# One block instead of two at the head of a two-layer hybrid kernel: vectors, turned inputs and the first modulated input

## The reference, cut to what matters

```python
def adaln(cv, w, b):
    return jax.nn.silu(cv) @ w + b

def modulate(x, shift, scale):
    return x * (1.0 + scale) + shift

def hgrn_lower_bounds(logits):
    p = jax.nn.softmax(logits.astype(jnp.float32), axis=0)
    return jnp.clip(jnp.cumsum(p, axis=0) - p[0], 0.0, 1.0)
...
    p_lat = jnp.split((h_lat @ w_in).astype(jnp.float32), split_at, axis=-1)
    p_ctx = jnp.split((h_ctx @ w_in).astype(jnp.float32), split_at, axis=-1)
```

## Time and profile before

| what | value |
|---|---|
| median of 3 runs | 4275.97 us (4269.83 to 4277.84) |
| profiled execution, its own time | 4269.11 us |
| its span, first to last instruction | 4267.2 us |
| mean granted TensorE clock over the span | 0.929 of full speed |
| PE busy | 3724.2 us, 87% |
| PEld (weight loads) busy | 3004.4 us, 70% |
| DVE busy | 1755.2 us, 41% |
| ACT busy | 1060.2 us, 25% |
| POOL busy | 231.3 us, 5% |

### The profile page before, as it was taken

The page is one execution under the profiler, slowest core; times in us unless marked ns, Lnnn a source line. Parts: engine busy times, 40 slices in busy tenths (PEclk is TensorE's granted clock), DMA queues, the critical chain, the costliest instruction groups (busy, mean ns, idle before and its releaser), DMA issues. The chain is left out here.

```text
span 4267.2 us, 52183 instructions
## 1 busy us (share of the span) xinstructions
PE 3724.2 (87%) x22306; PEld 3004.4 (70%) x22306; DVE 1755.2 (41%) x1933; ACT 1060.2 (25%) x1465; POOL 231.3 (5%) x126
## 2 busy tenths in 40 slices
PE   3999567979796999999998699568979869999997
PEld 2888445548785888888886588445458758888886
DVE  3111657655424323323334321667556243333334
ACT  1000232446405111111112300232456141111113
POOL 2000003002000000000000000003012000000000
PEclk6999778989898999999999899779989989999998
DMA  5532523022312111111112522422031311211111
GB/s 190 120 88 74 212 92 109 7 82 66 136 52 74 45 45 29 29 44 44 29 32 92 144 84 90 167 98 61 6 110 51 119 40 45 59 44 44 51 38 43
DMA packets 300024, 318.71 MB, mean 75 GB/s; under 512 B 42479, under 2 KB 266331, under 8 KB 299611
## 3 DMA queue, kind: packets, MB, share of 16 engines
q1 hardware_dynamic: 274234, 267.43, 21.1%
q0 software_dynamic: 6912, 30.15, 2.3%
q10 hardware_dynamic: 18720, 18.88, 1.3%
HBM read 247.78 MB, written 71.59 MB: 75 GB/s over the span
## 5 line engine op out<-in xcount | busy, mean ns | idle before, releaser
L491 PE MATMUL psum<-h_hi,f_whi 128*128 128x512 f32 (+1 forms) x1760 | 482.0, 371 | 43.2 <-DVE f_wlo L1114 43.2
L491 PE MATMUL psum<-h_lo,f_whi 128*128 128x512 f32 (+1 forms) x1760 | 481.3, 371 | 0.0
L491 PE MATMUL psum<-h_hi,f_wlo 128*128 128x512 f32 (+1 forms) x1760 | 481.3, 371 | 0.0
L491 PE MATMUL psum<-h_hi,w_hi 128*128 128x512 f32 (+1 forms) x1392 | 369.1, 368 | 99.0 <-DVE w_lo L636 67.8
L491 PEld LDWEIGHTS psum<-h_hi,f_whi 128*128 128x128 f32 x1760 | 308.7, 188 | 102.5 <-DVE f_wlo L1114 43.6
L491 PE MATMUL psum<-h_lo,w_hi 128*128 128x512 f32 (+1 forms) x1392 | 367.2, 367 | 0.0
L1120 DVE SCALAR_TENSOR_TENSOR y<-psum,mods,y 128x1024 f32<-128x1024 f32 (+1 forms) x264 | 260.4, 1015 | 258.4 <-PE psum L491 257.5
L491 PE MATMUL psum<-h_hi,w_lo 128*128 128x512 f32 (+1 forms) x1392 | 366.0, 366 | 0.0
L491 PEld LDWEIGHTS psum<-h_lo,f_whi 128*128 128x128 f32 x1760 | 308.5, 188 | 59.0
L491 PEld LDWEIGHTS psum<-h_hi,f_wlo 128*128 128x128 f32 x1760 | 308.4, 188 | 59.0
L491 PEld LDWEIGHTS psum<-h_hi,w_hi 128*128 128x128 f32 x1392 | 239.4, 190 | 146.0 <-issue 42.1
(11 more groups left out here) (267 smaller groups left out, 5295.6 us busy)
## 6 DMA issues: line engine op xcount, KB each, us to landing
f_raw<-in_w_ffn_in SPq DMA_DIRECT2D x88, 512.0 KB, 6.1
ada_w<-in_w_ada SPq DMA_DIRECT2D x30, 1024.0 KB, 10.9
w_raw<-in_w_in SPq DMA_DIRECT2D x48, 512.0 KB, 5.3
proj_cm<-lin_stage POOLq DMA_DIRECT2D x38, 640.0 KB, 4.2
f_raw<-in_w_ffn_out SPq DMA_DIRECT2D x44, 512.0 KB, 3.8
ada_w<-in_w_ada ACTq DMA_DIRECT2D x18, 1024.0 KB, 5.6
na_qk<-proj_cm SPq DMA_DIRECT2D x48, 320.0 KB, 8.0
hg_pj<-proj_cm SPq DMA_DIRECT2D x20, 640.0 KB, 8.8
```

The source lines that it names most:

```text
L491: ins = nc.tensor.matmul(out[:, t0:t0 + tn], w, h[:, t0:t0 + tn], start=start and n == 0, stop=stop and n == 2)
```

## The change

`setup` and `turn_in` become one function, `front`, with one block.

- SP issues the 16 small loads first (the identity third), then all ten tile loads (those from the fifth on wait for the transposes of the tile four before), then the stores, two tiles in each: five stores of 1024 KB.
- ACT issues the first four `w_ada` pieces at the start, ahead of its Exp and its Silu.
- PE makes the transposes of the vectors and `head_wide`, then waits for `s_done`, which DVE gives with `c_wide`; from there its list is the old one.
- DVE has the same small steps in another order: `head_mean` early, so that `head_wide`'s products run beside the other steps, and `head_wide` and `c_wide` last.
- The modulated input has three buffers, which lie in the memory of `x_rows`. DVE makes the even blocks (`tensor_scalar`), ACT the odd ones (`Identity` with scale and bias); ACT makes all `h_hi`, DVE all `h_lo`. POOL has nothing in the block.
- All semaphores of the block but those of `ModulationTiled` come from the pool.

The diff (the bodies of `setup` and `turn_in`, taken out, are printed above and are cut here, as are the counts at the end):

```diff
@@ -145,90 +145,6 @@
 V_ROWS = 94
-def setup(k):
...
 class Modulation:
@@ -394,45 +310,81 @@
...
-def turn_in(k, h_hi, h_lo, mod_ranges):
...
+def front(k, h_hi, h_lo, mod_ranges):
+    nc, a = k.nc, k.a
     ROWS_IN = 4
     with ExitStack() as st:
...
+        sem = k.stage_sems(st)
+        vec_rows = k.sb(st, "vec_rows", [V_ROWS, P])
+        ada = k.sb(st, "ada_rows", [DEPTH * MB, P])
+        tmp = k.sb(st, "lb_tmp", [P, 8, 4])
+        rows = k.sb(st, "x_rows", [P, ROWS_IN * D])
         xc = k.sb(st, "x_cm", [P, KB, NT])
-        hm = k.sb(st, "h_mod", [P, 2, NT])
         mod = ModulationTiled(k, st, 4, 5, mod_ranges)
         n_m = len(mod.pieces)
...
+        HM = 3
+        s_in = [sem(f"x_loaded{s}") for s in range(ROWS_IN)]
+        (s_con, s_vt, s_v, s_e, s_hm, s_hw, s_done, s_out, s_t, s_x, s_md, s_ma, s_hi, s_lo) = (sem(x) for x in (
+            "rows_loaded", "rows_turned", "vec_step", "lb_exp", "head_mean", "head_wide", "vectors_done", "x_stored", "x_turned", "x_copied",
+            "modulated_dve", "modulated_act", "h_hi", "h_lo"))
+        def row_tile(t):
+            return rows[:, t % ROWS_IN * D:(t % ROWS_IN + 1) * D]
+        def hm(j):
+            return rows[:, j % HM * NT:(j % HM + 1) * NT]
...
+        n = [0]
         with nc.Block() as block:
             @block.sync
             def _(sp):
                 def load(t):
                     if t >= ROWS_IN:
                         sp.wait_ge(s_t.h, s_t.at(t - ROWS_IN + 1))
...
+                    src = a["x"][0, t * P:(t + 1) * P] if t < SEQ // P else a["ctx"][0, t * P - SEQ:(t + 1) * P - SEQ]
+                    sp.dma_start(row_tile(t), src).then_inc(s_in[t % ROWS_IN].h, 16)
+                for dst, src in (
+                    (vec_rows[V_C:V_C + 8], a["c"].rearrange("a (j p) -> (a j) p", p=P)),
+                    (vec_rows[V_C + 8:V_C + 16], a["c_ctx"].rearrange("(j p) -> j p", p=P)),
+                    (k.ident[:], a["c_ident"]),
+                    (vec_rows[V_LNG:V_LNG + 32], a["ln_g"].rearrange("l w (j p) -> (l w j) p", p=P)),
+                    (vec_rows[V_LNB:V_LNB + 32], a["ln_b"].rearrange("l w (j p) -> (l w j) p", p=P)),
+                    (vec_rows[V_LBL:V_LBL + 8], a["hgrn_lb_logits"].rearrange("l d (j p) -> (l d j) p", p=P)),
+                    (ada[:], a["b_ada"].rearrange("l (j p) -> (l j) p", p=P)),
+                    (k.mean_d[:], a["c_mean_d"]), (k.mean_h[:], a["c_mean_h"]), (k.rot[:], a["c_rot"]),
+                ):
+                    sp.dma_start(dst, src).then_inc(s_con.h, 16)
+                for row, name in ((V_QN, "gqa_q_norm"), (V_KN, "gqa_k_norm"), (V_HN, "hgrn_norm")):
+                    for half in range(2):
+                        sp.dma_start(vec_rows[row:row + DEPTH, half * HD:(half + 1) * HD], a[name]).then_inc(s_con.h, 16)
+                for t in range(TT):
                     load(t)
...
-                    sp.wait_ge(s_x.h, s_x.at(t + 1))
-                    sp.dma_start(k.x_dram[:, :, t * P:(t + 1) * P], xc[:, :, t * P:(t + 1) * P]).then_inc(s_out.h, 16)
-                    if t + ROWS_IN < TT:
-                        load(t + ROWS_IN)
...
+                for t in range(0, TT, 2):
+                    sp.wait_ge(s_x.h, s_x.at(t + 2))
+                    sp.dma_start(k.x_dram[:, :, t * P:(t + 2) * P], xc[:, :, t * P:(t + 2) * P]).then_inc(s_out.h, 16)
+                sp.wait_ge(s_out.h, s_out.at(16 * TT // 2))
             @block.tensor
             def _(pe):
+                pe.wait_ge(s_con.h, s_con.at(16 * 16))
+                nc.tensor.transpose(k.psum[:, 0, 0:V_ROWS], vec_rows[:], k.ident[0:V_ROWS, 0:V_ROWS])
+                nc.tensor.transpose(k.psum[:, 1, 0:DEPTH * MB], ada[:], k.ident[0:DEPTH * MB, 0:DEPTH * MB]).then_inc(s_vt.h, 1)
+                pe.wait_ge(s_hm.h, s_hm.at(1))
+                for c in range(3):
+                    for i in range(4):
+                        ins = nc.tensor.matmul(k.psum[32 * c:32 * c + 32, 2, i * P:(i + 1) * P], k.head_mean[:, i], k.ident[:], start=True, stop=True)
+                ins.then_inc(s_hw.h, 1)
+                pe.wait_ge(s_done.h, s_done.at(1))
                 for t in range(TT):
...
+                    pe.wait_ge(s_in[t % ROWS_IN].h, s_in[t % ROWS_IN].at(row_copied(t)))
                     if t >= 2:
                         pe.wait_ge(s_x.h, s_x.at(t - 1))
                     for j in range(KB):
                         ins = nc.tensor.transpose(k.psum[:, 2 * (t % 2) + j // 4, (j % 4) * P:(j % 4 + 1) * P],
...
+                                                  row_tile(t)[:, j * P:(j + 1) * P], k.ident[:])
                     ins.then_inc(s_t.h, 1)
                     for u in range(n_m * t // TT, n_m * (t + 1) // TT):
                         mod.product(pe, u)
@@ -442,6 +394,39 @@
             @block.vector
             def _(dve):
+                def step(ins):
+                    ins.then_inc(s_v.h, 1)
+                    n[0] += 1
+                    dve.wait_ge(s_v.h, s_v.at(n[0]))
+                dve.wait_ge(s_vt.h, s_vt.at(1))
+                step(nc.vector.tensor_copy(k.vecs[:, 0:V_ROWS], k.psum[:, 0, 0:V_ROWS]))
+                lg = k.vecs[:, V_LBL:V_LBL + 8].rearrange("p (l q) -> p l q", l=DEPTH)
+                step(nc.vector.tensor_tensor(tmp[:, 4], lg[:, 0], lg[:, 1], ALU.max))
+                step(nc.vector.tensor_tensor(tmp[:, 0:2], lg, tmp[:, 4:5].to_broadcast([P, 2, 4]), ALU.subtract))
+                step(nc.vector.tensor_copy(k.b_ada[:], k.psum[:, 1, 0:DEPTH * MB]))
+                step(nc.vector.memset(k.head_mean[:], 0.0))
+                for i in range(4):
+                    ins = nc.vector.tensor_copy(k.head_mean[:, i, 2 * i:2 * i + 2], k.mean_h[:, 0:P:HD])
+                ins.then_inc(s_hm.h, 1)
+                step(nc.vector.memset(k.eps[:], EPS))
+                step(nc.vector.memset(k.eps_dn[:], EPS / ALPHA ** 2))
+                step(nc.vector.memset(k.c_wide[:], 0.0))
+                step(nc.vector.tensor_tensor(k.c_pick[:], k.ident[:, 0:2], k.ident[:, 32:34], ALU.add))
+                for g in range(2, 4):
+                    step(nc.vector.tensor_tensor(k.c_pick[:], k.c_pick[:], k.ident[:, 32 * g:32 * g + 2], ALU.add))
+                dve.wait_ge(s_e.h, s_e.at(1))
+                step(nc.vector.tensor_tensor(tmp[:, 4], tmp[:, 2], tmp[:, 3], ALU.add))
+                step(nc.vector.reciprocal(tmp[:, 5], tmp[:, 4]))
+                step(nc.vector.tensor_tensor(tmp[:, 0:2], tmp[:, 2:4], tmp[:, 5:6].to_broadcast([P, 2, 4]), ALU.mult))
+                step(nc.vector.tensor_tensor(tmp[:, 6], tmp[:, 0], tmp[:, 1], ALU.add))
+                step(nc.vector.tensor_tensor(k.lb[:, 0], tmp[:, 0], tmp[:, 0], ALU.subtract))
+                step(nc.vector.tensor_tensor(k.lb[:, 1], tmp[:, 6], tmp[:, 0], ALU.subtract))
+                step(nc.vector.tensor_scalar(k.lb[:], k.lb[:], 0.0, 1.0, ALU.max, ALU.min))
+                step(nc.vector.tensor_scalar(k.omlb[:], k.lb[:], -1.0, 1.0, ALU.mult, ALU.add))
+                dve.wait_ge(s_hw.h, s_hw.at(1))
+                step(nc.vector.tensor_scalar(k.head_wide[0:96].rearrange("p i m -> p (i m)"), k.psum[0:96, 2], float(HD), None, ALU.mult))
+                dve.wait_ge(s_e.h, s_e.at(2))
+                nc.vector.tensor_copy(k.c_wide[:, :, 0:2], k.vecs[:, V_C:V_C + 16].rearrange("p (t j) -> p j t", t=2)).then_inc(s_done.h, 1)
                 for t in range(TT):
                     dve.wait_ge(s_t.h, s_t.at(t + 1))
                     nc.vector.tensor_copy(xc[:, :, t * P:(t + 1) * P],
@@ -449,38 +434,73 @@
                 mod.finish(dve)
                 dve.wait_ge(mod.s_v.h, mod.s_v.at(mod.steps))
                 dve.wait_ge(s_x.h, s_x.at(TT))
+                def modulated(j):
+                    if j >= HM:
+                        dve.wait_ge(s_lo.h, s_lo.at(j - HM + 1))
+                    for c, (t0, t1) in enumerate(((0, SEQ), (SEQ, NT))):
+                        ins = nc.vector.tensor_scalar(hm(j)[:, t0:t1], xc[:, j, t0:t1], k.mods[:, 0, KB + j, c:c + 1],
+                                                      k.mods[:, 0, j, c:c + 1], ALU.mult, ALU.add)
+                    ins.then_inc(s_md.h, 1)
+                def lower(j):
+                    dve.wait_ge(s_hi.h, s_hi.at(j + 1))
+                    nc.vector.tensor_tensor(h_lo[:, j], hm(j), h_hi[:, j].bitcast(F32), ALU.subtract).then_inc(s_lo.h, 1)
+                modulated(0)
+                modulated(2)
                 for j in range(KB):
...
+                    lower(j)
+                    if j % 2 and j + 3 < KB:
+                        modulated(j + 3)
             @block.scalar
             def _(act):
                 for u in range(min(mod.RING, n_m)):
                     mod.load(act, u)
+                act.wait_ge(s_v.h, s_v.at(3))
+                nc.scalar.activation(tmp[:, 2:4], tmp[:, 0:2], ACT.Exp).then_inc(s_e.h, 1)
```

(77 more changed lines are left out.)

83 lines of the change are left out of this document (removed).

## The result

| | before | after |
|---|---|---|
| median | 4275.6 us (4269.83 to 4277.84, 4 runs) | 4242.65 us (4241.93 to 4244.11, 4 runs) |
| profiled execution | 4269.11, span 4267.2 | 4241.93, span 4240.5 |
| mean granted clock | 0.929 | 0.934 |

The ratio is 0.9925, interval 0.9913 to 0.9938: faster by 33 us of median. Forecast were 4239.0 and a range of 4227 to 4254. But the two profiled executions differ by 27.2 us only, and the head, which is all that the change edits, by 25.9. The forecast had 34.2 for it. So the total came out near the forecast by luck: its largest term was 8.3 us too good, and the difference was made up by something else.

What follows compares the result with a forecast made beforehand. The head was taken as three serial stretches: vectors, full DMA engines, modulated input. Starting the modulated input 22.1 us earlier and shortening it by 12.1 saves 34.2 us, from 4273.2 to 4239.0, range 4227 to 4254.

Steps and rivals of the forecast that it cites:

- What bounds the head: Head before the change: 18 us of vectors, 51 us of transfers and turning, 32 us of modulated input, one after another.
- The vectors: Start of the head: vectors land at 9.0, then 6.8 us of steps, so TensorE's tiles start at 15.8 instead of 22.04.
- after 12: Sign that the forecast is wrong: the vectors land later than 12 us.
- vectors land behind the weights: Rival: loads in flight go first, vectors at 20, tiles at 26.8, modulated input at 56; 25 us saved, chance 0.10.
- The loads' end: Piece and tile loads of the head end at 43.5, with 39.1 and 45 as ends; pieces at 191 GB/s from 8.5.
- The tail: From the last product's start to the modulated input: 3.3 us, so the modulated input starts at 46.8.
- The stores: Head's stores: 1.3 MB moved by 42.5, the other 4.0 MB by 53, covered; 10 us without that cover.
- The modulated input: Last stretch of the head: 20.0 us instead of 32.1 with VectorE and ACT sharing it, 12.1 us less.
- the rival in which they hinder each other: Modulated input: VectorE and ACT slow each other, 33 us, its 12 us of gain lost, 4252 us; chance 0.06.
- TensorE at its lower clock: Rival: TensorE paces the head at 43.4 us of work, modulated input at 60, 21 us saved, 4252 us; chance 0.13.
- The total: Whole kernel: 34.2 us saved in the head, everything behind it unchanged, 4239.0 us.
- five signs of being wrong: Vectors after 12, modulated start past 52, h_lo over 2 us, DMA hole around 20, mean clock below 0.925.

Runs made afterwards that it cites:

- e3: Changed kernel with head_wide's products behind tile 5, its copy behind tile 6, and c_wide made early; 4241.36 us.
- e1: Changed kernel with SP's first store waiting for the product of the last ada_w piece; 4240.51 us.
- e8: Changed kernel with stores behind the last piece, head_wide late, and tile transposes ahead of awaited pieces; median 4234.98 us, ratio 0.9909 to the kernel before.
- e7: Changed kernel with SP's old order: four tile loads, then each tile's 512 KB store and the load four after; 4247.44 us.
- e10: Changed kernel with ACT's first four piece loads issued behind Exp and Silu; 4243.83 us.
- e6: Changed kernel with two pieces issued at the start and the other two behind Exp and Silu; 4240.87 us.
- e9: The edits of e8 on the changed kernel, with only two pieces issued ahead of Exp and Silu; median 4237.46 us, ratio 0.9918.
- before_again: Kernel before the change, unchanged, profiled a second time; 4278.13 us.

## Why the prediction was right, and where it was not

**What bounds the head.** Right: three stretches in a row, DMA-bound in the middle, POOL-bound at the end.

**The vectors.** The forecast has 16 issues at 0.45 us done "until about 7", where its own price gives 8; they took until 7.27. The sum behind the landing was right, 6.8 us forecast and 7.0 measured from 12.60 to 19.59. The landing was mis-sized: 9.0 forecast, 12.60 measured, in a row that I had named as the sign of an error ("after 12"). The evidence that I leaned on, a tile that was there 3.95 us after its issue, was of a tile issued together with the pieces. The small loads are issued one after the other for 6 us, into engines that are already full, and TensorE needs the last of them. The rival "vectors land behind the weights" had the direction, but not the mechanism: at 12.60, ACT's queue had moved 2.85 of its first 4.19 MB, so not all in flight went first, and the landing is 4.7 us over the undisturbed 7.9, of the 12 that the rival had. That the rival's modulated input at 56 and gain of 25 us are what was measured is a coincidence; its tiles would have started at 26.8, and they started at 19.59.

**The loads' end.** This is the step that failed: 43.5 forecast, 51.8 measured. The forecast let the pieces run at half rate, 191 GB/s, without a break from 8.5 to 42.5, and added 1.0 us for ACT's queue being empty "for a moment". Up to 20 that was near: 1.95 MB by 8.5 (1.9 forecast), then 172 GB/s. Two things broke it.

- The hole. The tiles started 3.8 us later than I had them, so the buffers were full before TensorE emptied the first. It was both queues that ran empty. From 20 to 28 the pieces moved 0.48 MB where half the rate is 1.53; that is 5.5 us, against the 1.0.
- The stores' share. From 44 to 51.8 the stores moved 1.90 MB and the pieces 1.07, which is 137 GB/s and not 191, or 2.2 us. By 51.8 the stores had moved 3.0 MB, where the forecast had 1.3 by the loads' end.

The smaller shortfalls from 8.5 to 20 and from 28 to 44 (172 and 182 GB/s) make the other 1.9 us: 42.5 + 5.5 + 2.2 + 1.9 is within 0.3 of the 51.8. Closing the hole gives 3.2 us back and not 5.5 (e3, in which the stores start 4.5 us earlier and so run beside more of the pieces); taking the stores away gives 2.5 at the last product (e1).

TensorE's list, with tile 8 behind piece 5 and tile 9 behind piece 6, is no part of this miss: the four late pieces were all asked for by 31.30, and the last product still waited 0.76 us for its piece. It becomes the limit only when the stores wait, in e1. And that e8 wins 9.3 us, where the modulated input missed its 46.8 by 9.2, does not show that its edits undo just what the forecast missed: e8 also takes away stores whose share was in the forecast's 43.5.

**The tail.** 4.2 us instead of 3.3 from the last product, at the lower clock, whose price I had at 3.9. The 3.9 is short because two pieces are turned at the end, not one: eight passes, 1.87 us at the lower clock and 1.17 before.

**The stores.** Covered as forecast: the DMAs are empty from 60 on, 15 us before the block's end. That their share of the bandwidth slows the pieces was in the sum, but at half, and it was more. e1 prices the whole of it at 2.5 us up to the last product, and the clock behind that at 1.6.

**The modulated input.** 20.0 forecast, 19.1 measured, 32.1 again with POOL back. The 0.9 us less come from ACT, whose instructions follow each other closer than their own lengths: 1.73 us for a modulated block with parts of 1.237 and 0.585. VectorE beside ACT kept its 1.09 for a block (1.13 later on), so the rival in which they hinder each other is out.

**TensorE at its lower clock.** Not the pace of the head. It did however begin slowly in the first profile: 16 transposes in 3.68 us, where the run again has 1.97. Product 0 is 1.7 us later for it, and the modulated input 1.6. From 36.6 to 41.0 TensorE waited for a piece, and the granted clock was 1.00 up to 40, 0.58 from 40 to 42 and 0.50 from there to 56, with short waits for pieces in between. In e7, where from 48.4 on it waited for no DMA, it was 0.50 up to 52, 0.88 from 52 to 54 and then 1.00, and the last product took 1.07 us instead of 1.94. The Trainium skill, "TensorE: Matmul & The Clock Gate", Part 1, says that activity releases the throttled state and that an idle TensorE falls back to it. The fall after the wait and the rise in e7 agree; in the kernel after the rise did not come by 56.

**The total.** 34.2 us of gain in the head were forecast and 25.9 came. I took it from 4273.2, the mean of the executions known, and the kernel before has its median at 4275.6 in that comparison and at 4277.0 and 4274.3 in two others. The rest of the program gave 1 us between the two profiled executions and about 7 between the medians. The 4239.0 is only 3.7 us off because a miss of 8.3 us was made up for by something that no step of the forecast had. That is luck. Of the five signs of being wrong that the forecast named, three came: the vectors after 12, a modulated start past 52, and the hole.

## What to carry to other kernels

Issuing loads first pays only as far as there are buffers: count what fits in them, and see whether the consumer is awake when they are full; small transfers that the consumer waits for can go ahead of the bulk, where here they landed 4.7 us earlier and nothing was lost (e10). A store without a deadline still takes bandwidth from the loads, here 64% of it at the end, so let it wait for the last load. Then look at the consumer's own list: in e1 two tiles that had their data stood behind products that were waited for. And check a forecast by its steps: here the total was right and the largest step was not.

## What the hardware showed unexpectedly

- Sixteen small loads with 0.36 MB landed at 7.9 alone (five runs), at 11.52 and 11.70 with two pieces of 1 MB issued beside them (e6, e9) and between 11.90 and 12.60 with four (seven runs). The issue itself was hardly slower: the last ended at 7.27 instead of 6.90.
- The granted clock that a trace shows ahead of its first change is not to be trusted: from 20 to 22 it reads 1.00 in the kernel after, while its 16 transposes took 3.68 us, the same work that took 1.97 in another run of it. In before_again it reads 1.00 from 20 to 28, while eight transposes took 1.97 us twice, where eight take 1.09 at full clock.
- One program on one core takes 4267 to 4281 us, and 2.7 of 8 us of such a difference lay in one stretch of 150 us, at 0.86 instead of 0.89 of the clock.
- The rate of loads alone was not one number: 388 GB/s with tiles and pieces, but 355 over the first 18 us of the kernel after, in which the small loads ran among them, with 327 to 350 from 6 to 12, and 386 to 405 from 12 to 18, when the small ones were through.
